# DeltaNet recurrence in a two-layer hybrid decoder: key and query times the state in one product with a 128-column stationary, and one more projection tile spread over the recurrence's waits

## The reference

```python
h = rms_norm(x, norm1_g[l]); proj = h @ w_in[l]          # 6832 columns, cut into the mixers' inputs
a_u, a_v, q_lat, kv_lat, k_rope, c_qkv, c_z, c_b, c_a, gates = jnp.split(proj, split_points, axis=-1)
...
def step(state, inp):                                     # once per chunk, in order
    q_i, k_i, u_i, w_i, a_i, g_i = inp
    v_new = u_i - einsum('bhck,bhkv->bhcv', w_i, state)
    o = (einsum('bhck,bhkv->bhcv', q_i * exp(g_i)[..., None], state)
         + einsum('bhcs,bhsv->bhcv', a_i, v_new))
    g_last = g_i[..., -1]
    state = state * exp(g_last)[..., None, None] + einsum('bhck,bhcv->bhkv', k_i * exp(g_last[..., None] - g_i)[..., None], v_new)
    return state, o
...
o = rms_norm(o, o_norm_g) * silu(c_z)                     # then @ w_branch[2], times sigmoid(gate), summed over the mixers
```

## Time and the profile before

| | |
|---|---|
| time before, 3 runs | 1837.96 us median, 1836.77 to 1838.29 |
| the profiled execution | 1838.14 us, span 1836.3 us from first to last instruction (1.8 us around it) |
| PE busy | 1810.2 us, 99% of the span |
| mean granted TensorE clock | 0.998 of full speed |
| POOL / DVE / ACT busy | 1030.2 / 859.3 / 463.3 us |
| DMA | 167.31 MB, mean 91 GB/s |

### The profile page before, as it was taken

One profiled execution on the slowest core, in us unless ns is written; L12 is line 12 of the kernel. 1 busy time (PEld: TensorE's weight loads), 2 busy tenths in 40 slices (PEclk: granted clock), 3 DMA queues, 4 the chain that ended last, 5 costly groups with the idle time before them and its releaser, 6 DMA issues.

```text
span 1836.3 us, 26908 instructions
## 1 busy us (share of the span) xinstructions
PE 1810.2 (99%) x10374; PEld 1485.4 (81%) x10374; DVE 859.3 (47%) x1347; ACT 463.3 (25%) x866; POOL 1030.2 (56%) x580
## 2 busy tenths in 40 slices
PE   8999999999999999999999999999999999999998
PEld 7887788778888888888888777877788888888887
DVE  8686536663454232314365945366544351414141
ACT  6423316550122000000244233165411130001010
POOL 6534367235666666666653524652456666666662
PEclk9999999999999999999999999999999999999999
DMA  6212133123223323233342211221323323223331
GB/s 232 88 60 79 36 93 104 45 92 92 92 92 108 102 92 103 92 104 92 99 132 68 69 59 58 92 92 36 115 81 94 102 92 99 96 94 101 92 103 69
DMA packets 46762, 167.31 MB, mean 91 GB/s; under 512 B 5018, under 2 KB 8346, under 8 KB 46146
## 3 DMA queue, kind: packets, MB, share of 16 engines
q1 hardware_dynamic: 44066, 154.50, 26.6%
q10 hardware_dynamic: 2592, 11.29, 1.6%
HBM read 159.47 MB, written 6.29 MB: 90 GB/s over the span
## 4 chain that ended last, share of the span: by engine, by line
PE 93%; DVE 4%; ACT 1%; issue 1%; DMA 0%; SPq 0%; ACTq 0%; DVEq 0%
PE ps L444 27%; PE ps L445 27%; PE ps L446 27%; PE ps L907 2%; PE ps L916 1%; PE ps L929 1%; PE ps L534 1%; DVE acc L1462 1%; PE ps L679 1%; PE ps L711 1%; PE ps L689 1%; DVE r L1753 1%; DVE hLo L1455 0%; PE ps L592 0%; PE ps L997 0%
## 5 line engine op out<-in xcount | busy, mean ns | idle before, releaser
L412 POOL TENSOR_TENSOR wLo<-wraw,wHi 128x1024 fp32r<-128x1024 f32 x288 | 722.6, 2509 | 23.9
L407 POOL TENSOR_SCALAR wHi<-wraw 128x1024 fp32r<-128x1024 f32 x288 | 307.6, 1068 | 754.2 <-PE ps L446 738.2
L444 PE MATMUL ps<-hHi,wHi 128*128 128x512 f32 x1360 | 554.8, 408 | 0.4 <-DVE convd L1582 0.4
L446 PE MATMUL ps<-hHi,wLo 128*128 128x512 f32 x1360 | 530.5, 390 | 0.0
L445 PE MATMUL ps<-hLo,wHi 128*128 128x512 f32 x1360 | 530.5, 390 | 0.0
L444 PEld LDWEIGHTS ps<-hHi,wHi 128*128 128x128 f32 x1360 | 255.8, 188 | 59.8 <-issue 6.0
L445 PEld LDWEIGHTS ps<-hLo,wHi 128*128 128x128 f32 x1360 | 256.2, 188 | 55.1 <-issue 4.6
L446 PEld LDWEIGHTS ps<-hHi,wLo 128*128 128x128 f32 x1360 | 255.7, 188 | 54.4
L444 PE MATMUL ps<-fHi,wHi 128*128 128x512 f32 x640 | 249.3, 389 | 0.0
L446 PE MATMUL ps<-fHi,wLo 128*128 128x512 f32 x640 | 249.0, 389 | 0.0
L445 PE MATMUL ps<-fLo,wHi 128*128 128x512 f32 x640 | 249.0, 389 | 0.0
(11 more groups left out here) (308 smaller groups left out, 1982.3 us busy)
## 6 DMA issues: line engine op xcount, KB each, us to landing
wraw<-stream SPq DMA_DIRECT2D x288, 512.0 KB, 3.5
out<-xT ACTq DMA_DIRECT2D x2, 2048.0 KB, 9.5
xT<-out ACTq DMA_DIRECT2D x2, 2048.0 KB, 9.0
xin<-x SPq DMA_DIRECT2D x4, 512.0 KB, 6.3
out<-ost ACTq DMA_DIRECT2D x1, 1024.0 KB, 4.1
out<-ost ACTq DMA_DIRECT2D x2, 512.0 KB, 3.8
prm<-params ACTq DMA_DIRECT2D x1, 647.0 KB, 3.9
prm<-params SPq DMA_DIRECT2D x1, 576.0 KB
```

The lines of the kernel that those rows point to most:

```text
L407: nc.gpsimd.tensor_scalar(wHi[:, slot], wraw[:, slot % RAW], 1.0, 0.0, ALU.mult, ALU.add).then_inc(unit_high, 1)
L412: nc.gpsimd.tensor_tensor(wLo[:, slot], wraw[:, slot % RAW], wHi[:, slot].bitcast(F32), ALU.subtract).then_inc(unit_split, 1)
L444: mm(o, lh[lc], rh[rc], start=start, stop=False)
L446: return mm(o, ll[lc], rh[rc], start=False, stop=stop)
```

## The change

The key and the query of a chunk become one stationary of 128 columns (64 key, 64 query, in an order by the chunk's parity), multiplied with the state once per step; its result fills all 128 partitions of a bank of its own for each parity and step (`chunk_bank`), the query part on the half opposite to the key part (`query_rows`), and `chunk_output` accumulates there. L701 and its semaphore go. A step of tile av2 stands between L689 and the wait for vnew in steps 1 to 7, its last step in the first wait of step 8; the whole tile after the recurrence goes. The transposes of the four token tiles move: 0 into the second wait of step 8, 1 and 2 into gate2 tile 0, 3 into the middle of gate2 tile 1. DVE makes `kqe` of odd chunks by two instructions of half the width, and ACT copies krope after all five latent squares. (Two hunks that only take away the name `query_done` are left out.)

```diff
--- before.py
+++ after.py
@@ -369,6 +369,14 @@
         def turned_probs(h):
 
             return probT[:, h % 6] if h % 6 < 4 else probU[:, h % 6 - 4]
+
+        def chunk_bank(step, par):
+
+            return ps[:, 2 + 4 * (step % 2) + par]
+
+        def query_rows(m):
+
+            return np.s_[64 - 64 * (m % 2):128 - 64 * (m % 2)]
 
         def sums_bank(d):
 
@@ -672,16 +680,21 @@
                     if step == 0:
                         pe.wait_ge(corner_placed, layer * per.corner_placed + 3)
                     else:
+                        if step == 1:
+                            pe.wait_ge(corner_placed, layer * per.corner_placed + 5)
+                        if step >= 2:
+                            pe.wait_ge(o_copied, layer * per.o_copied + step - 1)
                         pe.wait_ge(state_done, layer * per.state_done + step)
                         for j in range(PAIRS):
                             for par, m in both:
                                 if m:
-                                    last = mm(S(2)[hs(m), j * 64:j * 64 + 64], kqe[cs(par), j, m // 2, m % 2, 0], state[cs(par), j], start=True, stop=True)
+                                    last = mm(chunk_bank(step, par)[:, j * 64:j * 64 + 64], kqe[cs(par), j, m // 2, m % 2].rearrange("p k s -> p (k s)"),
+                                              state[cs(par), j], start=j == 0, stop=False, skip_group_check=True)
                         last.then_inc(ws_done, 1)
                         if step < CHUNKS:
                             project(("av", 1), range(step, step + 1))
                         else:
-                            turn_delta_output(0)
+                            project(("av", 2), range(KD - 1, KD))
                         pe.wait_ge(r_ready, layer * per.r_ready + step)
                     for j in range(PAIRS):
                         for par, m in both:
@@ -691,17 +704,10 @@
                     last.then_inc(tr_done, 1)
                     if step == 0:
                         project(("av", 1), range(0, 1))
-                    if step == 1:
-                        pe.wait_ge(corner_placed, layer * per.corner_placed + 5)
-                    if step >= 2:
-                        pe.wait_ge(o_copied, layer * per.o_copied + step - 1)
-                    for j in range(PAIRS):
-                        for par, m in both:
-                            if m:
-                                last = mm(S(step % 2)[hs(m), j * 64:j * 64 + 64], kqe[cs(par), j, m // 2, m % 2, 1], state[cs(par), j],
-                                          start=j == 0, stop=False, skip_group_check=True)
-                    if step:
-                        last.then_inc(query_done, 1)
+                    elif step < CHUNKS:
+                        project(("av", 2), range(step - 1, step))
+                    else:
+                        turn_delta_output(0)
                     pe.wait_ge(vnew_done, layer * per.vnew_done + step + 1)
                     if step < CHUNKS:
                         for j in range(PAIRS):
@@ -714,7 +720,7 @@
                     if step == 0:
                         pe.wait_ge(corner_placed, layer * per.corner_placed + 5)
                     else:
-                        pe.wait_ge(query_done, layer * per.query_done + step)
+                        pe.wait_ge(ws_done, layer * per.ws_done + step)
                     chunk_output(step)
 
                 def chunk_output(step):
@@ -722,13 +728,15 @@
                     for j in range(PAIRS):
                         for par, m in chains(step):
                             hs = np.s_[64 * (m % 2):64 * (m % 2) + 64]
-                            last = mm(S(step % 2)[hs, j * 64:j * 64 + 64], gated[hs, m // 2, 1, 2 * j + par], vnew[hs, step % 2, j],
+                            last = mm(chunk_bank(step, par)[query_rows(m), j * 64:j * 64 + 64], gated[hs, m // 2, 1, 2 * j + par], vnew[hs, step % 2, j],
                                       start=m == 0 and j == 0, stop=j == PAIRS - 1, skip_group_check=True)
                     last.then_inc(o_done, 1)
 
                 def turn_delta_output(tt):
 
                     pe.wait_ge(on_done, layer * per.on_done + tt + 1)
+                    if tt < 2:
+                        pe.wait_ge(o_copied, layer * per.o_copied + CHUNKS)
                     if tt >= 2:
                         pe.wait_ge(oval_ready, layer * per.oval_ready + tt - 1)
                     for j in range(PAIRS):
@@ -740,9 +748,9 @@
                     for d2 in range(4):
                         if d2 == 0 and first == 0:
                             project((f"gate{br}", 0), range(0, 2))
+                            turn_delta_output(1)
+                            project((f"gate{br}", 0), range(2, 6))
                             turn_delta_output(2)
-                            project((f"gate{br}", 0), range(2, 6))
-                            turn_delta_output(3)
                             project((f"gate{br}", 0), range(6, KD))
                         elif d2 == 0 and first == 1:
                             project((f"gate{br}", 0), range(2, KD))
@@ -751,7 +759,12 @@
                         if d2 == 0 and first == 1:
                             sum_av()
                             pe.wait_ge(inv_copied, layer * per.inv_copied + 4)
-                        project((f"gate{br}", 2 * d2 + 1))
+                        if d2 == 0 and first == 0:
+                            project((f"gate{br}", 1), range(0, 4))
+                            turn_delta_output(3)
+                            project((f"gate{br}", 1), range(4, KD))
+                        else:
+                            project((f"gate{br}", 2 * d2 + 1))
                         if d2 == 0:
                             pe.wait_ge(b_lo, layer * per.b_lo + (2, 6, 10)[first])
                         u = UNIT_NO[(f"y{br}", d2)]
@@ -838,8 +851,6 @@
                 corner_products()
                 for step in range(CHUNKS + 1):
                     recur(step)
-                turn_delta_output(1)
-                project(("av", 2))
                 branch_out(2, 0)
 
 
@@ -1212,12 +1223,12 @@
                 act.wait_ge(act_tile, layer * per.act_tile + 12)
                 square_lat(0)
                 square_lat(1)
-                act.wait_ge(kr_turned, layer * per.kr_turned + 1)
-                nc.scalar.copy(krope[:], S(4)[:, 0:TT * ROPE].rearrange("p (t r) -> p t r", t=TT)).then_inc(kr_copied, 1)
                 square_lat(2)
                 act.wait_ge(kqe_done, layer * per.kqe_done + 8)
                 for j in range(3, 5):
                     square_lat(j)
+                act.wait_ge(kr_turned, layer * per.kr_turned + 1)
+                nc.scalar.copy(krope[:], S(4)[:, 0:TT * ROPE].rearrange("p (t r) -> p t r", t=TT)).then_inc(kr_copied, 1)
                 take_z(0)
                 act.wait_ge(lsq_step, layer * per.lsq_step + 1)
                 nc.scalar.copy(lsums[:, 0:SEQ], S(2))
@@ -1266,7 +1277,7 @@
                     for par, m in chains(step):
                         rows = np.s_[64 * (m % 2):64 * (m % 2) + 64]
                         ins = nc.scalar.copy(o_tm[rows, m // 2].rearrange("p (j q v) -> p j q v", j=PAIRS, q=2)[:, :, par],
-                                             S(step % 2)[rows, 0:256].rearrange("p (j v) -> p j v", j=PAIRS))
+                                             chunk_bank(step, par)[query_rows(m), 0:256].rearrange("p (j v) -> p j v", j=PAIRS))
                     ins.then_inc(o_copied, 1)
                     if step and step % 2 == 0:
                         square_o(step // 2 - 1)
@@ -1601,8 +1612,14 @@
                 def scale_pair(m):
                     ch, j = m % 2, m // 2
                     dve.wait_ge(qk_exp, layer * per.qk_exp + m + 1)
-                    tt_(kqe[:, j, :, ch].transpose([0, 2, 1, 3]), kqT[:, :, j].rearrange("p k (t c s) -> p k t c s", t=TT, c=2)[:, :, :, ch],
-                        S(2 + m % 2).rearrange("p (t k s) -> p k t s", t=TT, k=2), ALU.mult).then_inc(kqe_done, 1)
+                    vectors = kqT[:, :, j].rearrange("p k (t c s) -> p k t c s", t=TT, c=2)[:, :, :, ch]
+                    rows = S(2 + m % 2).rearrange("p (t k s) -> p k t s", t=TT, k=2)
+                    if ch == 0:
+                        ins = tt_(kqe[:, j, :, 0].transpose([0, 2, 1, 3]), vectors, rows, ALU.mult)
+                    else:
+                        for kind in range(2):
+                            ins = tt_(kqe[:, j, :, 1, 1 - kind], vectors[:, kind], rows[:, kind], ALU.mult)
+                    ins.then_inc(kqe_done, 1)
 
                 for i in range(9):
                     conv(i)
@@ -1751,7 +1768,7 @@
                             if m:
                                 hs = np.s_[64 * (m % 2):64 * (m % 2) + 64]
                                 ins = tt_(r[hs], rhsv[hs, m // 2].rearrange("p (j q v) -> p j q v", j=PAIRS, q=2)[:, :, par],
```

(6 more changed lines are left out.)

## The result

The changed kernel takes 1846.28 us (median of 5 runs, 1845.43 to 1848.71), the kernel before beside it 1838.19 (5 runs, 1836.77 to 1839.12). The ratio is 1.0047, 95% interval 1.0032 to 1.0062: slower by 0.47%, some 8.1 us. The forecast was 1839.4, its range ended at 1844.5, and "slower" had a chance of 22%.

The account below looks back on a forecast made before the run. PE, busy 99% of the span, bounds the kernel. Per layer +5.96 (recurrence) - 4.59 (tile leaving) + 0.5 (bLo) - 1.40 (krope) + 0.17 (kqe) = +0.64, +1.3 for two on 1838.14: 1839.4 us, range 1833.0 to 1844.5.

Parts of the forecast that it names:

- Wait A: Recurrence step, first start of L679 to L689: 1.64 to 2.04 us, +0.40; in step 8 PE's floor of 1.90, +0.71.
- cheap: Rival on the 128-column load: 0.058 us a record, nothing extra, total 1833.0 us, faster by 0.3%; chance 18%.
- one stream after the other: Rival on the new product: both parities' streams don't run together, last start 1.71, total 1849.6 us; chance 9%.
- load and product in turn: Rival on the new product: within one stream they don't overlap, 0.165 us a record, total 1846.8 us; chance 4%.
- Wait B: Recurrence step, L689 to L711: with a step of av2 in it bound by PE, 1.15 to 1.50 us, +0.35.
- Step 8 and the end: Last recurrence step until gate2's first product: 2.67 us after L689, total change there -4.59 us a layer.
- the stall on avT: After the recurrence, gate2 waits for its bank, av1's, until DVE has read it: PE stalls 0.8 us.
- the stall on bLo: Ahead of y2, PE waits for bLo behind the last transpose group: +0.5 us; rival 1.4 us under POOL's split, 7%.
- The krope copy: Ahead of the recurrence, with ACT's copy last PE's idle time before L826 goes: -1.40 us a layer, nothing late instead.
- The halves of kqe: Ahead of the convolution, two half-width DVE instructions for odd chunks, 0.86 us for 0.68: +0.17 a layer.
- wait C: Recurrence step, L711 to the next L679: unchanged at 1.20 us, the new o_copied wait met a full step earlier.
- the clock: Rival: one low-clock window of three us more or fewer, costing 1.5 us: 1837.9 or 1840.9 us, 7% together.

Follow-up runs that it names:

- The moved wait: Changed kernel with PE's wait for o_copied moved from in front of the state wait to ahead of the av2 step: 1844.59 us, ratio 1.0040.
- The late negation: Changed kernel with DVE's negation of headstat put after the two scalings of turned heads that PE waits for: 1841.66 us, ratio 1.0022.
- the product alone: Changed kernel without av2 steps in the recurrence (whole tile after it) and with transposes back in their old places: 1846.99 us, ratio 1.0080.
- The first pair above: Changed kernel with its waits, negation, av1 read and fourth transposes reordered, 128-column product whole against cut into halves: 1838.34 and 1832.44 us.
- the pair with equal clocks: Changed kernel with only the negation after the scalings, 128-column product whole against cut into halves: 1841.66 and 1837.33 us.

## Why the prediction was wrong, by its steps

**Right.** Wait A: forecast 2.04 and 1.90, measured 2.05 and 1.90; the load of 128 columns sets the pace (0.111 a record in the trace, 0.107 taken), two streams run beside each other, and L691 to r is 1.15 for 1.13. Two readings behind it were loose without harm: the earlier trace rows are products of 32 rows and not of 64, and the 0.46 of eight records are one interval of 0.11 and six of 0.058. The three rivals on the load fell with it (cheap, one stream after the other, load and product in turn), and with the last of them the rule of the Trainium skill ("TensorE: Matmul & The Clock Gate", Part 3, The mechanism) that the prediction names beside it. Load and product of one row group in turn would be 0.165 a record, the trace shows 0.111. Wait B: 1.50, bound by PE. Step 8 and the end: L702 to gate2's first product 2.70 for 2.67, the stall on avT 0.83 for 0.8, the stall on bLo 0.36 for 0.5. The krope copy: -1.47 for -1.40, and nothing was late in its place.

**Too dear.** The halves of kqe cost 0.05 and 0.09, not 0.17: DVE waits for PE in that stage.

**Wrong: wait C.** The step said "unchanged", and that the new wait for `o_copied` "is met a full step earlier". It is met; but it stands as a second wait ahead of one instruction, and that costs an instruction after the state has come: +0.09 to 0.10 in each of eight steps, 0.8 a layer, 1.6 us in all. The moved wait gave it back. With it the changed places sum to +1.47 and +1.54 for the +0.64 a layer forecast, +3.0 us for +1.3.

**Wrong: the rest of the kernel was taken as fixed.** DVE's negation and POOL's wLo were within 0.4 us of each other in layer 0 of the kernel before, and I had read only the contention on bLo, not this one. DVE now reaches that place 1.47 us later (318.08 for 316.61), POOL's wLo only 0.77 (317.76 for 316.99), and the negation falls into it: 1.5 us of PE that the sum has at nothing. The page of waits before showed the same stall in layer 1 (1.8 us), which should have been a rival. The late negation took it away in both layers.

**Wrong: the end of the output was taken as fixed.** The sum went from the time before by what PE does, with the last transfer and the 1.8 us around the span as they were. From ACT's last copy to the end are 7.55 us in the profiled execution for 5.98 before, 1.6 more, with a piece of q8 beside the transfer.

**Under-sized: the clock.** I gave it one window in either direction. The profiled execution had one more than before, and across the runs the changed kernel's mean granted clock is 0.9966 where before has 0.9984, some 3.3 us at the lower level's price. That is more than PE lost: the mean also counts the last low stretch, behind PE's last product, which lasts 5.0 and 3.4 us in the changed kernel's two profiles for 2.1 before, so 0.6 to 1.5 of the 3.3 cost nothing. Part of the rest comes with the stall: of the twelve stalls at the heads in the profiles, four have a low stretch right behind them (three of five in layer 0, one of seven in layer 1), and no kernel without the stall has one there. Part may come with the wide product: stretches in the recurrence or right behind it stand in three of seven profiles with it and in none of seven without, and the product alone, with nothing in wait B, had runs 20 us over its best. The first pair above speaks for it, the pair with equal clocks against; I count this as possible and not as shown.

**The account**, against the kernel before: ring, end, kqe and krope +3.0; one more stall at the heads 1.5, and what low stretch comes with it about 1; the end of the output 1.2 on average, 1.6 in the profiled execution. That is 6.7 to 7.1 of the 8.1 us, and the 1.0 to 1.4 left are about what one low stretch more in most runs would cost. **Open**: at what a low stretch that isn't behind a stall begins, and whether the piece of q8 alone makes the end late.

## What to carry to other kernels

In a ring of hand-overs count records by what each stream loads, not by how many there are: a wide stationary with few moving columns takes the load's time, and two narrow ones in different columns run beside each other. Give the instruction on the critical hand-over one wait only, and put the others where PE waits for nothing. Before adding or taking a microsecond, look at where two engines start within half a microsecond of each other later on: what DVE does between SBUF and SBUF may fall into an instruction of POOL, and an order that keeps such work behind what PE waits for does not depend on the phase. Compare the last transfer of both kernels, and what else the DMA queues do beside it, before the whole difference is put down to the edit.

## What the runs showed of the hardware that was not expected

- A second semaphore wait ahead of a PE instruction: 0.051 us as an instruction of its own, 0.09 to 0.10 on the ring, though its condition had long been met.
- 64x64 products into both column halves: 32 records in 0.98 us, with the next full-size product 0.91 after the first; 16 records of 64x128 take 1.11, the next 1.04 after the first.
- A DVE instruction of 128x32 from SBUF to SBUF, 0.17 to 0.35 us alone, took 2.07 to 2.38 when it started up to 0.32 us after POOL's wLo (2.35 us long) in either of two forms, and 0.47 when it started 1.93 after it; it ended with wLo each time, within 0.05 us; two DVE scalings that read PSUM took 2.56 beside wLo and 2.46 without.
- A stretch of 3.4 us at the granted clock of 0.5 costs 1.6 us. Such stretches sit at different places in different executions of one kernel, but some places come again: of the 18 in the fourteen profiles (without those at the very end) seven are at 974 to 979 us, four at 68, and four right behind a stall of PE of 1.5 us or more.
- A piece of 16 KB of an instruction list on its way beside the output's last two transfers: these took 5.0 to 5.4 us from issue to landing in three profiles, and 3.7 to 3.9 in the eleven where none was there.
